# Forty projection slices laid anew among the samples' RWKV products of a hybrid decoder layer

## The reference, cut to what matters

```python
def step(S, inp):
    r_t, w_t, k_t, v_t, kk_t, a_t = inp
    sk = jnp.einsum('bhij,bhj->bhi', S, kk_t)
    S = S * w_t[:, :, None, :] - sk[..., None] * (kk_t * a_t)[:, :, None, :] + v_t[..., None] * k_t[:, :, None, :]
    return S, jnp.einsum('bhij,bhj->bhi', S, r_t)
...
o = ((o - mean) * lax.rsqrt(var + LN_X_EPS)).reshape(B, T, RWKV_WIDTH) * W['rwkv_ln_gain'] + W['rwkv_ln_bias']
...
proj = h @ W['w_in']
```

## Time and profile before

| | us |
|---|---|
| runs of the kernel before | 1732.47, 1735.99, 1736.41 (median 1735.99) |
| the profiled execution, its own time | 1736.48 |
| its span, first to last instruction | 1734.6 |
| PE busy in the span | 1681.9 (97%) |
| mean granted TensorE clock | 0.99 |

### The profile page before, as it was taken

The page is one execution under the profiler, slowest core; times in us unless marked ns, Lnnn a source line. Parts: engine busy times, 40 slices in busy tenths (PEclk is TensorE's granted clock), DMA queues, the critical chain, the costliest instruction groups (busy, mean ns, idle before and its releaser), DMA issues.

```text
span 1734.6 us, 41459 instructions
## 1 busy us (share of the span) xinstructions
PE 1681.9 (97%) x16564; PEld 1602.0 (92%) x16564; DVE 953.0 (55%) x1484; ACT 737.8 (43%) x1226; POOL 710.2 (41%) x912
## 2 busy tenths in 40 slices
PE   6899999999899999999999999999999899999999
PEld 6899999999799999998788989898999899999999
DVE  6836547366854545454475362727455945637363
ACT  5544536355523333332243443435334553536442
POOL 4554645555322222121132323324255573645643
PEclk9999999999899999999899999999999999999999
DMA  5353433423332334232055453446463352343512
GB/s 183 121 186 110 133 110 122 157 85 136 142 138 77 105 117 146 89 102 71 32 212 186 172 186 145 165 157 238 143 228 121 130 193 95 116 148 112 192 61 107
DMA packets 57497, 237.30 MB, mean 137 GB/s; under 512 B 7520, under 2 KB 8160, under 8 KB 55904
## 3 DMA queue, kind: packets, MB, share of 16 engines
q1 hardware_dynamic: 49440, 218.35, 35.7%
q10 hardware_dynamic: 7872, 16.37, 2.5%
HBM read 216.93 MB, written 71.76 MB: 166 GB/s over the span
## 4 chain that ended last, share of the span: by engine, by line
PE 85%; DVE 9%; ACT 2%; issue 1%; DVEq 1%; POOL 0%; DMA 0%; ACTq 0%
PE ps L396 29%; PE ps L825 23%; PE ps L835 16%; PE ps L1428 4%; PE ps L2375 1%; PE ps L2550 1%; PE ps L2475 1%; PE ps L2419 1%; PE ps L2497 1%; DVE T_lo L964 1%; PE ps L2459 1%; DVE B_lo L964 1%; PE ps L2490 0%; ACT w_hi L376 0%; DVE hf L1748 0%
## 5 line engine op out<-in xcount | busy, mean ns | idle before, releaser
L383 POOL TENSOR_TENSOR w_lo<-w_raw,w_hi 128x256 fp32r<-128x256 f32 x384 | 320.1, 864 | 685.4 <-ACT w_hi L376 685.4
L396 PE MATMUL ps<-h_hi,w_hi 128*128 128x288 f32 x1232 | 289.2, 316 | 19.5 <-POOL w_lo L383 13.9
L396 PE MATMUL ps<-h_hi,w_lo 128*128 128x288 f32 x1232 | 265.2, 297 | 0.0
L396 PE MATMUL ps<-h_lo,w_hi 128*128 128x288 f32 x1232 | 264.8, 297 | 0.0
L396 PEld LDWEIGHTS ps<-h_hi,w_hi 128*128 128x128 f32 x1232 | 200.1, 191 | 41.6 <-POOL w_lo L383 14.5
L396 PEld LDWEIGHTS ps<-h_lo,w_hi 128*128 128x128 f32 x1232 | 200.0, 190 | 0.0
L396 PEld LDWEIGHTS ps<-h_hi,w_lo 128*128 128x128 f32 x1232 | 199.5, 190 | 0.0
L808 POOL TENSOR_TENSOR ring_lo<-raw,ring_hi 128x256 fp32r<-128x256 f32 (+1 forms) x197 | 147.3, 772 | 112.3 <-ACT ring_hi L789 111.5
L376 ACT ACTIVATE w_hi<-w_raw 128x1024 fp32r<-128x1024 f32 x96 | 101.7, 1060 | 107.9 <-PE ps L396 93.6
L825 PE MATMUL ps<-T_hi,ring_hi 128*128 128x288 f32 x396 | 118.4, 299 | 11.1 <-ACT u L1052 8.7
L1235 DVE SCALAR_TENSOR_TENSOR x<-ps,x 128x576 f32<-128x576 f32 x64 | 48.5, 758 | 139.5 <-PE ps L835 138.2
(11 more groups left out here) (454 smaller groups left out, 3975.2 us busy)
## 6 DMA issues: line engine op xcount, KB each, us to landing
w_raw<-in_w SPq DMA_DIRECT2D x122, 512.0 KB, 3.4
raw<-in_w SPq DMA_DIRECT2D x48, 512.0 KB, 4.9
kv<-in_kc SPq DMA_DIRECT2D x32, 576.0 KB, 6.6
kv<-in_vc SPq DMA_DIRECT2D x32, 576.0 KB, 7.3
cache_out<-in_cache SPq DMA_DIRECT2D x28, 576.0 KB
raw<-in_w_down SPq DMA_DIRECT2D x32, 384.0 KB, 3.4
w_raw<-in_w_down SPq DMA_DIRECT2D x16, 384.0 KB, 3.7
gates<-gate_out ACTq DMA_DIRECT2D x16, 288.0 KB, 2.3
```

The source lines that it names most:

```text
L383: last = nc.gpsimd.tensor_tensor(w_lo[par_][:, c], w_raw[par_][:, c], w_hi[par_][:, c].bitcast(F32), ALU.subtract)
L396: last = nc.tensor.matmul(ps[:, b + c, 0:HC], w[par_][:, wk], a[:, k, c * HC:(c + 1) * HC], start=(first and k == 0), stop=(end and k == n ...
```

## The change

Only the calls of `fill` in `rwsam_pe` change. No slice is added or dropped: five leave their old places, and five go to new ones. ACT, DVE, POOL and SP keep their lists as they are.

- The fill of 6 ahead of the first `s_inv` wait becomes 4, the fill of 3 ahead of the second becomes 2, and of the last three fills the two of 3 become 2 each.
- A single slice is laid in the middle of run A and one in the middle of run B (at the third head pair, after 32 of 64 products), and one behind each run.
- The fill ahead of the sixth `s_dve` wait grows from 2 to 3.

The fills are then: 2, 4, 2, 2, 3, 2, 2, run A with 1 inside, 1, 2, 3, run B with 1 inside, 1, 3, 3, 2, 2, 2, 2.

```diff
@@ -1989,7 +1989,7 @@
             scores(6, 1, 0)
             ln_var(pe, 0)
-            fill(6)
+            fill(4)
             pe.wait_ge(sem("s_inv"), 1)
             heads(4, mm(SLM), mm(SXT))
             fill(2)
@@ -1997,7 +1997,7 @@
             ln_gate(pe, 0)
-            fill(3)
+            fill(2)
             pe.wait_ge(sem("s_inv"), 2)
@@ -2024,10 +2024,13 @@
             for ct, b, h in ((ct, b, h) for ct in range(CT) for b in range(DB) for h in range(2)):
+                if (ct, b, h) == (2, 0, 0):
+                    fill(1)
                 c = slice(64 * ct + 8 * b, 64 * ct + 8 * b + 8)
...
             last.then_inc(sem("smat"), 1)
+            fill(1)
             ln_gate(pe, 1)
             ln_centre(pe, 2)
             fill(2)
```

## The result

The changed kernel takes 1754.44 us (median of 4, 1752.56 to 1756.48) against 1735.86 for the kernel before in the same comparison: a ratio of 1.0102, 95% interval 1.0089 to 1.0115, some 17.7 us. Its profiled execution took 1754.30 with a span of 1752.5, 17.9 more than the span of before. The forecast was +6.3 on the profiled execution of before, 1743.0, and a range to 1748.0. The sign was right, and the size was short by nearly a factor of three.

The account below looks back on a forecast made before the run. PE, holding 85% of the chain that ended last, was taken to bound the kernel. +5.4 at full clock less 3.9 for the old falls gave +1.5; new falls +4.8 made +6.3, stated as 1743.0 us, range 1737.0 to 1748.0.

Parts of the forecast that it names:

- The ACT stalls: PE waiting on ACT behind unit 0's and unit 1's evacuations: 1.43 us, then some 0.7 and 2.5 us idle.
- The tail: Last fills of the stage, two slices removed: only the first shortens the chain, -0.79 us, not -1.58.
- The full-clock sum: Whole stage, both kernels at full clock: 3.95 - 0.15 - 0.79 - 0.79 + 3.2 = +5.4 us.
- before's falls: Two clock drops around runs A and B in the kernel before: 3.9 us, the most steadying the clock gives back.
- Units 2, 3 and 4: Later units' evacuations and weight splits on ACT and POOL: no cost from their new ends, 0 us.
- unit 1's end: Last slice of unit 1 now just ahead of heads(7), so its evacuation delays take(11) and run A: +3.2 us.
- the clock afterwards: TensorE clock falls in the changed stage: 2.5 us at run A, 1.8 at run B, 0.5 at the first stall; +4.8.
- Rival 3: Stalls come and the clock stays low through both runs and following norm matmuls: +9.3 to near +11, 1746 to 1748; chance 0.13.

Follow-up runs that it names:

- ACT's list mended: Changed kernel, PE's list kept; on ACT raw_out(0) moved behind take(3), raw_out(1) and next_hi(1) behind take(11): 1.0024 of the kernel before, +4.2 us.
- second attempt: Changed kernel with three slices inside each run, ACT's first two evacuations behind the takes, two slices at each wait just ahead of run A: 1.0022 of before, +3.8 us.
- first attempt: Changed kernel with three slices inside each run, ACT's first three evacuations moved back, thinner fills ahead of run A, two slices behind run B's centre: 1.0014 of before, +2.4 us.
- kernel with both stalls: Kernel before with only the changed kernel's early fills, three slices moved to the sixth s_dve wait, none inside the runs, tail as before: 1.0075, +13.0 us.

## Why the prediction was right in its waits and wrong in its size

**The ACT stalls: right, to 0.2 us.** Reckoned 1.43, measured 1.4. Reckoned "some 0.7 and then 2.5", measured 0.8 and 2.3. What made them computable is that ACT's order is written out, and that each step in the block had its duration in a row.

**The tail: right.** One of its two slices came back as a wait (0.5 us at the last gate), and from the fourth spread product to attention's first own slice the chain is 0.9 us shorter (8.36 for 9.26), for 0.79 reckoned. PE waited for the first spread as before (0.5, where 0.6 or more was said).

**The full-clock sum, +5.4, +1.5 with before's falls given back: short by some 0.9 us.** "Units 2, 3 and 4 ... Nothing there: 0" is a term that was not nothing. Unit 3 does end a fill earlier, but that brings POOL's work on the next weights on top of DVE's last spread rows, and costs the 0.8 us shown above. It happens in all six profiled executions in which the two overlap (the changed kernel twice, and once with ACT's list mended; slices in the runs without the stalls; three slices; the second attempt), and in none of the five others, where the pair takes 1.3 us. At full clock a slice amid 8-column products and 32 of those also take 0.98 + 1.03 = 2.01 us (first attempt, 834.13 and 835.12), 0.3 more than 0.79 + 32 x 0.029; in the changed kernel that lies within the low stretches, and is no term of its own in the sum below. Two readings were off by 0.2 each and cancel: the centre behind a gate takes 0.86 at full clock (858.23 in the chain of the changed kernel), not 1.05, so before's falls cost 4.1 and not 3.9, and unit 1's end cost some 3.4 and not 3.2.

**The step that failed is "the clock afterwards", +4.8 taken, with 2.5 + 2.5 + 1.4 = 6.4 as the upper bound.** By the chain above, the low stretches of the changed kernel cost:

- behind the first stall: two groups of heads 2.92 for 2 x 1.07, gate 2.00 for 1.05, two slices 2.88 for 1.58. Sum 3.0, where 0.5 was taken and 1.4 was the bound;
- through run A: heads 0.79, first half 3.35 - 1.80, second 3.52 - 1.86, two slices 0.95 each, gate 0.65. Sum 6.55, where 2.5 was taken and was also the bound;
- from run B's slice on: 0.50, 1.66, 0.95, 0.67. Sum 3.8, where 1.8 was taken and 2.5 was the bound.

That is 13.3 for 4.8. With it the working gives 1.5 + 13.3 = 14.8, with the 0.8 of DVE's spread 15.6, and the stage grew by 15.7.

Two errors lie in it. *The price*: what run B lost in before, 1.53 us at 42 ns an instruction, was taken as the most that a run can lose. The 42 ns were a mean over a run that was partly at full clock: its window says 0.79. At 1.2 GHz the price is 55 ns, nearly twice the 29 of full clock, and run A whole at that level lost 3.2 us (1.55 + 1.66), not 1.5. *The length*: the two falls of before, 3.4 and 6.8 us long, were taken as what a fall is. But a low stretch has no fixed length: in the stages profiled here they lasted from 3.4 to 17.1 us, and the second of the changed kernel was 13.7 us in one execution and 17.1 in the other. What sets the length, these runs don't show. Rival 3 had named that mechanism, with a chance of 0.13, but priced it by the same two falls, and so the range ended at 1748.

The Trainium skill's rule (TensorE: Matmul & The Clock Gate, HAM oscillation) that gaps bring the clock down is borne out in part: the clock fell behind both stalls. But they are shorter, 1.4 and 2.3 us, than the gap its rule asks for, 64x64 or 8-column products stood around each of them, and in before and in the first attempt the clock fell with no stall at all.

**The intent of the change** failed too. One slice in the middle of a run does not hold the clock (+3.8 without any ACT stall). Three did in one profiled execution, and then waits on DVE behind run B, 3.0 us longer than in before, took most of what was given back, 0.8 us of it through POOL.

## What to carry to other kernels

Filler work that is counted off in units is tied to other engines: before you move it, count where each unit now ends, and read what stands behind its evacuation in the next engine's written order. Follow an earlier end as well: what it starts on a third engine can run beside work on the chain, and cost it 0.8 us here. Price a fall of TensorE's clock from rows that are wholly at the lower level, never from a mean over a stretch that has both, and allow for long ones: a stall of 1 to 3 us ahead of thin matmuls cost two to three times itself here. Three moved lines on ACT gave back 12 of 17 us here, so look for the mend in the waiting engine's list before touching PE's.

## What the runs showed of the hardware that was not expected

A busy PE did not by itself end the lower clock. In the kernel with both stalls PE was busy for all of 848 to 856 us and at 1.2 GHz for all of it; slices and 8-column products by turns in the first attempt (1.74 and 1.81 us) left it low as well. In the kernel with three slices in each run the same alternation ran at full clock, 1.00 from 838 to 846. So the same sequence was seen at both levels. What decides between them, these runs don't settle.

An 8-column matmul costs 29 ns at 2.4 GHz and 55 at 1.2 GHz: its price nearly doubles, as that of a 512-column gate does (1.05 to 2.00 us), although it streams so few columns. And the two stalls, of 1.4 us and of 0.8 and 2.3 us, cost two to three times their own length.

DVE's products of 64x512 float32 elements took 0.68 us apiece with POOL at rest, and 0.96 and 1.20 beside POOL's subtraction (L383); POOL's four instructions took 3.7 to 3.8 us there, for 2.8 at their shortest. Not every DVE instruction beside POOL is slower. In the kernel before, POOL works from 874.71 to 878.07, and in that time L2314, which reads the product out of `ps`, takes 0.69 us, as it does elsewhere, while L2316, which reads no `ps`, takes 1.03 for 0.69. The stages of the other traces show the same: beside POOL, instructions that read `ps` kept their time, and nearly all that read none took longer. By what the two engines hinder each other no trace here shows.
